# Moving the normalised inputs by 32 bytes and the gate products by 128 in SBUF

## What is computed

```python
def _prenorm(h, gain, shift, scale):
    return _rmsnorm(h, gain) * (1.0 + scale) + shift

def _swiglu(h, w_in, w_out):
    g, u = jnp.split(h @ w_in, 2, axis=-1)
    return (jax.nn.silu(g) * u) @ w_out
...
h = h + 0.5 * g1 * _swiglu(_prenorm(h, norm_ffn1[layer], sh1, sc1), ffn1_w_in[layer], ffn1_w_out[layer])
...
u = h @ w_in                                   # second model: inputs of the four branches
proj = jnp.einsum('bsnc,ncd->bsnd', ys, w_branch)
```

## Time and profile before

| | us |
|---|---|
| median of 3 runs | 3036.04 (3035.89 to 3038.37) |
| span of the profiled execution | 3035.4 |
| TensorE matmuls busy | 2979.4 (98%) |
| TensorE weight loads busy | 2629.2 (87%) |
| VectorE busy | 1691.5 (56%) |
| ScalarE busy | 1314.2 (43%) |
| DMA, mean over the span | 145 GB/s |

### The profile page before, as it was taken

One profiled execution on the slowest core, in us unless ns is written; L12 is line 12 of the kernel. 1 busy time (PEld: TensorE's weight loads), 2 busy tenths in 40 slices (PEclk: granted clock), 3 DMA queues, 4 the chain that ended last, 5 costly groups with the idle time before them and its releaser, 6 DMA issues.

```text
span 3035.4 us, 52037 instructions
## 1 busy us (share of the span) xinstructions
PE 2979.4 (98%) x20172; PEld 2629.2 (87%) x20172; DVE 1691.5 (56%) x2664; ACT 1314.2 (43%) x1952; POOL 0.2 (0%) x4
## 2 busy tenths in 40 slices
PE   8999999999999999999999999999999999999999
PEld 6778878787777878888889999999899999998998
DVE  4333363544332453334666667677766676787666
ACT  4322333423222332223345555555654554556544
POOL 0000000000000000000000000000000000000000
PEclk9999999999999999999999999999999999999999
DMA  9564342055576433333324655455456645554564
GB/s 276 174 185 133 115 146 82 30 167 167 172 212 184 132 100 88 110 90 92 110 71 117 188 167 158 144 155 166 133 159 181 180 124 163 155 155 142 155 183 129
DMA packets 639011, 439.36 MB, mean 145 GB/s; under 512 B 22172, under 2 KB 627192, under 8 KB 638712
## 3 DMA queue, kind: packets, MB, share of 16 engines
q1 hardware_dynamic: 637844, 436.70, 48.3%
q10 hardware_dynamic: 996, 0.23, 0.0%
HBM read 430.84 MB, written 1.05 MB: 142 GB/s over the span
## 4 chain that ended last, share of the span: by engine, by line
PE 88%; DVE 7%; ACT 2%; issue 1%; SPq 1%; DMA 1%; DVEq 0%; ACTq 0%
PE ps L453 27%; PE ps L455 26%; PE ps L454 26%; PE ps L541 2%; DVE wlo L402 2%; ACT whi L396 1%; PE ps L1803 1%; PE ps L1771 1%; DMA raw<-ffn_w_in 1%; DVE normed L2666 1%; PE ps L1791 1%; SPq L717 1%; DVE xl L2658 0%; PE ps L1252 0%; PE ps L1261 0%
## 5 line engine op out<-in xcount | busy, mean ns | idle before, releaser
L453 PE MATMUL ps<-xh,whi 128*128 128x256 f32 (+1 forms) x3744 | 1218.3, 325 | 23.1 <-DVE wlo L402 5.1
L454 PE MATMUL ps<-xl,whi 128*128 128x256 f32 (+1 forms) x3744 | 1197.2, 320 | 0.0
L455 PE MATMUL ps<-xh,wlo 128*128 128x256 f32 (+1 forms) x3744 | 1197.1, 320 | 0.0
L402 DVE TENSOR_TENSOR wlo<-raw,whi 128x1024 fp32r<-128x1024 f32 x732 | 868.9, 1221 | 186.9 <-ACT whi L396 178.2
L396 ACT ACTIVATE whi<-raw 128x1024 fp32r<-128x1024 f32 x731 | 746.5, 1052 | 472.2 <-PE ps L455 412.6
L453 PEld LDWEIGHTS ps<-xh,whi 128*128 128x128 f32 x3744 | 713.8, 191 | 105.3 <-issue 43.4
L455 PEld LDWEIGHTS ps<-xh,wlo 128*128 128x128 f32 x3744 | 714.0, 191 | 50.8
L454 PEld LDWEIGHTS ps<-xl,whi 128*128 128x128 f32 x3744 | 714.7, 191 | 48.8
L453 PE MATMUL ps<-hid_h,whi 128*128 128x512 f32 (+1 forms) x1056 | 355.9, 337 | 0.0
L454 PE MATMUL ps<-hid_l,whi 128*128 128x512 f32 (+1 forms) x1056 | 354.9, 336 | 0.0
L455 PE MATMUL ps<-hid_h,wlo 128*128 128x512 f32 (+1 forms) x1056 | 354.8, 336 | 0.0
(11 more groups left out here) (380 smaller groups left out, 2595.4 us busy)
## 6 DMA issues: line engine op xcount, KB each, us to landing
raw<-ffn_w_in SPq DMA_DIRECT2D x176, 512.0 KB, 4.6
mod_w<-ada_w SPq DMA_DIRECT2D x72, 1024.0 KB, 7.5
raw<-w_in SPq DMA_DIRECT2D x96, 512.0 KB, 4.5
raw<-w_ffn_in SPq DMA_DIRECT2D x88, 512.0 KB, 4.7
raw<-w_gate SPq DMA_DIRECT2D x64, 512.0 KB, 4.0
raw<-ffn_w_out SPq DMA_DIRECT2D x64, 384.0 KB, 4.0
raw<-ffn_w_out SPq DMA_DIRECT2D x64, 320.0 KB, 3.6
raw<-w_branch SPq DMA_DIRECT2D x32, 512.0 KB, 3.4
```

What stands on the lines that cost most here:

```text
L402: nc.vector.tensor_tensor(wlo[:, s, h, :], raw[:, s, h, :], whi[:, s, h, :].bitcast(F32), ALU.subtract).then_inc(S("lo_ready"), 1)
L453: nc.tensor.matmul(dst, w_h, x_h, start=start, stop=False)
L454: nc.tensor.matmul(dst, w_h, x_l, start=False, stop=False)
L455: return nc.tensor.matmul(dst, w_l, x_h, start=False, stop=stop)
```

## The change

Addresses are changed and nothing else. 32 bytes are left free ahead of xh, 32 behind xl, 64 ahead of hid_h and 64 behind hid32.

```diff
         hT = fixed("hT", [P, DC, 2 * T])
+        fixed.at += 32
         xh_at = fixed.at
         xh = fixed("xh", [P, DC, 2 * T], F32R)
         xl_at = fixed.at
         xl = fixed("xl", [P, DC, 2 * T], F32R)
-        overlay = fixed.at
-
-        first = Region(overlay)
+        overlay = fixed.at + 32
+
+        first = Region(overlay + 64)
         hid_h = first("hid_h", [P, max(HALVES), 2 * T], F32R)
         hid_l = first("hid_l", [P, max(HALVES), 2 * T], F32R)
         act32 = first("act32", [P, 2, 2 * T])
         hid32 = first("hid32", [P, 2, 2 * T])
+        first.at += 64
         out_at = first.at
...
-        e_xl = Region(xl_at, overlay)("e_xl", [P, DC, 2 * T])
+        e_xl = Region(xl_at, overlay - 32)("e_xl", [P, DC, 2 * T])
```

## The result

The changed kernel takes 3046.82 us, the median of 6 runs (3042.89 to 3050.76); the kernel before, run beside it, takes 3036.12 (3035.6 to 3038.37, 6 runs). The ratio is 1.0031, with a 95% interval of 1.0021 to 1.0041: slower by about 0.3%, 10.7 us. The forecast was 3004.3, in a range from 2984 to 3034. The profiled execution took 3045.37 us, with a span of 3043.6.

The account below looks back on a forecast made before the run. TensorE's step from one matmul start to the next was taken as the bound; gains of (23.1 + 10.4) x 0.946 = 31.7 us off the median 3036.04 gave 3004.3 us, range 2984 to 3034.

Parts of the forecast that it names:

- Term 1: The 8544 matmuls of 256 columns with xh or xl: each from 120.0 to 117.3 ns, a gain of 23.1 us.
- Term 2: The 3840 matmuls of 512 columns with xh or xl: 2.7 ns less each, a gain of 10.4 us.
- slower: Streamed rows beginning inside a 64 byte block cost 6.7 ns, less 2.7 won: 47 us lost, 3083 us; chance 0.07.
- Term 3: The 3168 hid matmuls: no change, as the phase by 64 bytes stays; bounds 8.6 us either way.
- Term 4: The 768 matmuls streaming h_yh and h_yl: no change, bounds 2.1 us.
- Term 5: ScalarE and VectorE writing xh and xl at the new phase, and transfers into mod_w: no change, at most 1.5 us lost by the writers.
- The factor: Share of the faster matmul steps that reaches the end: 2398 of 2535 us lie on the chain, 0.946.
- The base reading: TensorE's matmuls set the time: full clock steps carry 13.3 ns beyond their columns, h_yh 10.6, half clock none.
- Only the narrow gain: Only matmuls of 256 columns gain, 512 stay at 226.7 ns: 21.9 us, 3014 us; chance 0.16, shared with a partial gain.
- Much more: xh loses most of its 13.3 ns extra, or hid gains too: 78 us (2958) to 156 us (2880); chance 0.11.

Follow-up runs that it names:

- the kernel with the loss alone: Against the kernel before, xh and xl lie 32 bytes later only in the stages with 512 columns; 3059.21 us, ratio 1.0071.
- the one with the gain alone: Against the kernel before, xh, xl, hid_h and hid_l lie 32 bytes later only in the stages with 256 columns; 3010.95 us, ratio 0.9923.
- the fastest: Against the kernel before, xh, xl, hid_h and hid_l lie 192 bytes later only in the stages with 256 columns; 3001.7 us, ratio 0.9891.

## Why the prediction failed, step by step

**Term 1**, the 8544 matmuls of 256 columns, came out: 23.1 us forecast, 21.1 + 1.7 = 22.8 measured. The mechanism was right in that the distance to the weights counts. That the size fits is in part luck. It was taken over from h_yh because 160 and 32 are at the same phase by 64 bytes, and that phase is not what counts: 96 has it too, and hid there steps at 120.0, with no gain at all. The values are near each other and not the same: xh at 32 steps at 116.7 or 117.8, the weights at -32 at 118.3, h_yh at 160 at 117.3.

**Term 2** is the step that failed: "I take 2.7, since the extra of 13.3 is the same at both widths, so that its cause is likely the same for each matmul". It forecast a gain of 10.4 us on the 3840; they lost 24.3, and the kernel with that part alone is 21.8 us slower. The equal extra, 32 cycles at 2.4 GHz at either width, was read as one price for one cause. The table of distances shows that it is a value of two different curves that happen to meet at distance 0: 512 + 32 cycles is the lowest of one, 256 + 32 the highest of the other, among the distances tried. At 32 the first goes to 512 + 48 (233.3 ns) and the second to 256 + 24 (116.7). The text said that no row showed such a stream at another phase, and the bounds then taken, 0 and a gain of 51, left out a loss for this term, though the rival "slower" had priced just that, 6.7 ns. Why the two widths go opposite ways is not settled by any run here.

**Term 3**, hid at nothing "since the phase by 64 bytes does not change", failed as well. At 128 hid lost 10.0 us at 512 columns and won 2.1 at 256. Its bound, 2.7 ns either way, was too narrow: 6.3 came. The phase does not count modulo 64. That 256 is a full turn is shown by the kernel with xh and xl moved, where hid lay 256 bytes further on and stepped at 226.7 and 120.0 as before.

**Term 4**, h_yh: 0 forecast, 0.6 us lost, inside its bound. Even that need not be its move: at 160, as before, its mean goes from 117.4 to 118.3 in the other kernels. **Term 5**, writers and transfers: VectorE 1691.5 and 1691.7 us busy, ScalarE 1314.2 and 1313.9; nothing, as forecast. **The factor** 0.946 is of the right kind: 21.8 of 24.3 us reached the end in the kernel with the loss alone, and 25.3 of 26.4 in the one with the gain alone.

**The base reading** held: TensorE's step bounds the kernel, and in the stretches seen at either clock the address changes it at the full clock alone. At half clock the step of 256 columns stayed what it was in the earlier trace rows, and that of 512 columns is 426.7 ns both at distance 0 and, in the kernel with the loss alone, at 32. PE's timeline in the changed kernel, 15 steps in 3.20 us:

```profile
2490.85 0.41 PE L456 MATMUL ps<-xl,whi 128*128 128x256 f32 x1
...
2494.05 0.41 PE L456 MATMUL ps<-xl,whi 128*128 128x256 f32 x1
```

213.3 ns, at a granted clock of 0.50. The rule of the Trainium skill that the prediction weighed, "TensorE: Matmul & The Clock Gate", Part 2, on two independent read ports, is not borne out here as the prediction took it, that no address could matter: the step at full clock goes from 226.7 to 234.3 and from 113.3 to 120.0 by address alone. That it is the read of the stream and the read of the weight load that meet is a reading of the distances and was not shown; every matmul of `three` has its weight load, and no kernel was run without. What in the chip makes the distance count, no trace here shows.

**The rivals.** The time moved the way of "slower", and at 512 columns its 6.7 ns came; but it had both widths lose, 47 us in all, and 256 columns won. Its reason is refuted: the block of 64 bytes touched in its middle costs nothing when all buffers are shifted together (226.7), and hid at 128, on a whole block, pays it. "Only the narrow gain" had the right asymmetry, with a zero where a loss belonged. "Much more" is in part real, at a distance that wasn't the one chosen: 113.3 at 192, half the extra.

## What to carry to other kernels

Where TensorE runs matmul after matmul with a weight load each, place the streamed operands at a chosen distance from the weights, and choose it for each width apart: here one change of addresses won 25 us at 256 columns and lost 34 at 512. Read it from start to start in a long stretch without waits, and don't take a number seen at one width to the other, even if both show the same extra. When a term of a sum has no row of its own kind, its bounds go to both sides of zero.

## What the runs showed of the hardware that was not expected

- The matmuls of a stretch fall into a rhythm that lasts. At one distance two are possible, 113.3 and 117.8 ns at 192 and 116.7 and 117.8 at 32, and in one stage the rate went from 113.3 to 117.8 at a start that came 0.25 us after its forerunner. The same late start in two other layers of that execution left the rate at 113.4, so what picks the rate is not known.
- The rhythm belongs to the whole sequence. With `wlo` alone out of place, the starts behind matmuls that don't touch it come late too (238.4 and 232.4 ns), and the mean of the sequence is that of both weights out of place (233.2 at 512 columns, 118.3 at 256).
- The times of kernels with two possible rates spread more: 7.9 us over 6 runs of the changed kernel, 11.0 over 4 runs of the fastest and 8.5 over 5 of the one with 32 bytes in the 256 wide stages, against 2.8 over 6 and 3.6 over 9 of the one before and 3.7 over 5 of the one with the loss alone. That the choice of rate at each stretch's start makes this spread is likely, and was not shown: only one execution of each kernel has a trace.
- Sign matters: 32 bytes ahead of the weights is 116.7 to 117.8 ns at 256 columns, 32 behind is 118.3.
